# Eight adaLN modulation blocks: from TensorE in the attention to VectorE in the input projection

## The chip, the cores and the metric

The kernel runs on one core of one Trainium2 chip. The metric is the time of one execution on the device in microseconds (us). A trace is the record of one execution by the hardware profiler; its times are counted from its first instruction.

## The reference, cut to what matters

Two layers work on 256 latent tokens (and 256 context tokens that layer 0 alone reads), with 2048 features, in float32. Each sub-layer is modulated and gated by six vectors of 2048 that come from the conditioning vector `c`:

```
m_lat = split(silu(c) @ ada_w[i] + ada_b[i], 6)      # ada_w[i] is 2048 x 12288, 100.7 MB
hn    = modulate(rms_norm(h, norm1_g[i]), m_lat[0], m_lat[1])
h     = h + m_lat[2] * mixer_or_conv(hn)             # layer 0: attention + RWKV-7, layer 1: convolution
h     = h + m_lat[5] * mlp(modulate(rms_norm(h, norm2_g[i]), m_lat[3], m_lat[4]))
```

In layer 0 the mixer projects `hn` with one 2048 x 6560 matrix (`mix_in_w`), runs eight attention heads and sixteen RWKV heads on the result, and projects back with `mix_out_w`. The product `silu(c) @ ada_w` has one row. It is made here in blocks of 512 columns, 24 blocks per layer; a block is 2048 x 512 weights, 4.19 MB. Blocks 8 to 15 of layer 0 are `m_lat[2]` (the mixer's gate) and `m_lat[3]` (the second shift).

## The kernel before, in words

The kernel is one hand-ordered program: each engine (TensorE, VectorE, ScalarE, GpSimd, SyncE) has its own list of instructions in a fixed order, and semaphores tie the lists together. SyncE's list (`block.sync`) issues the weight loads, in order.

**The input projection.** `mix_in_w` is cut into 13 matrices of 512 columns, m0 to m12 (the last has 416), and each into four chunks c0 to c3 of 512 rows (1.05 MB). This text calls one chunk of one matrix a slot and writes (m, c). For each slot SyncE loads the chunk into `raw`, ScalarE rounds it (`split_hi`, line 410), VectorE makes the rest (`split_lo`, line 422), and TensorE multiplies (line 445, 48 matmuls to a slot). m0 and m1 need two of the four token groups (24 matmuls a slot). m6 and m7 need only the 256 latent tokens, and so do the last rows of m12. The hi and lo buffers hold one matrix: the rounding of chunk c of matrix m+1 waits until TensorE has finished slot (m, c). In the code's loops over m and c, VectorE therefore does the split of (m+1, c) in its own slot (m, c), beside TensorE's slot (m, c+1). After its four slots VectorE empties PSUM banks 2 and 3 of matrix m to `stage` (line 2700), and ScalarE banks 0 and 1 (line 2557). From m4 on ScalarE then issues the four stores of `stage`; two of them wait for VectorE's copies, and the next rounding stands behind them in ScalarE's list.

**Modulation blocks on VectorE.** Sixteen blocks (layer 0's 16 to 23, then layer 1's 0 to 7; `ADA_M`) are made beside the projection. A block is 16 pieces of 128 x 512. SyncE loads a piece (`load_piece`, line 739) into one of six buffers (`piece`: four in `gate`, two in `tmpa`), and a buffer is free when VectorE has used the piece before. VectorE multiplies it by one scalar per partition and adds it to an accumulator in `line` (`piece_step`, lines 749 and 752). `STEP_RATE[m]` says how many pieces VectorE does behind the split in each slot of matrix m. When a block's 16 pieces are done, TensorE sums the accumulator over the partitions (`sum_rows`, four matmuls at line 713) into a PSUM bank of the next matrix's half, and ScalarE copies the row and stores it to `mod_scratch` in DRAM (`keep_rows`, lines 767 and 718). `M_SUM` gives the slot before which TensorE does this: the first one after the slot that follows the block's last piece, at c1 or c2. TensorE waits there for the pieces (`macc_ok`), in order with its products.

Where VectorE also works on q and k: for m0 to m3 it normalises and turns the rows (`turn_sums`, `turn_rows`) in the first slots of the matrix behind.

**Attention.** Eight heads follow, one per pass n of a loop, pipelined across the engines (`attention`). In pass n TensorE makes the scores of head n (line 2876), transposes the maps of head n-1 (2888), multiplies them with the values (2901), and transposes k and q of head n+1 (2863, 2866). VectorE takes the maxima (2718), copies half of the transposed maps (2745), and makes the maps (2731, 2737), the queries (2712) and the outputs (2750, 2754). ScalarE does the exponentials (2583), the other half of the maps (2591), keys (2575), squares and a root (2597, 2605). Between these, TensorE makes one modulation block per pass (`weights`, line 382: 16 matmuls from `raw`, four per chunk): blocks 8 to 15 of layer 0. Chunks 0 and 1 stand ahead of the transposes of the maps, chunk 2 ahead of the values, chunk 3 behind the transposes of k and q. ScalarE copies the four partial rows of each and stores them (`act_ada`, lines 400 and 402). SyncE loads one 1.05 MB chunk at a time, when TensorE has used the one before (line 368).

`PARTED` names the two vectors whose sums lie in DRAM as four partial rows: their readers (`load_mod_rows`, `gate_part`, on GpSimd's queue) load or add four rows and not one.

Of the kernel before, what the change touches and what calls it, by code (L numbers as in the profile page):

```python
# [20 lines left out]
NB = 512  # L21
# [108 lines left out]
MIX_M = 13  # L130
ADA_A, ADA_T = 8, 1
ADA_M, M_BUF = 16, 6
ADA_L, L_BUF = 16, 3
Q_AT = ADA_A
Q_ALL = Q_AT + ADA_T * HEADS
SCAN = [[0, 1, 2, 3], [1, 0, 3, 2]]
# [99 lines left out]
def build_trunk(nc, a, out):  # L236
    with ExitStack() as top:
# [88 lines left out]
        mrow_zero = sem("mrow_zero")  # L326
        PARTED = [(0, 2), (0, 3)]
        late_in = [sem(f"late_in{b}") for b in range(L_BUF)]
# [26 lines left out]
        def weight_src(mat, col, n=NB, row=0):  # L355
            return mat[bass.ds(row, D), bass.ds(col, n)].rearrange("(k p) n -> p k n", p=P)
# [302 lines left out]
        def gate_part(pool, n, l, c, g):  # L659

            pool.wait_ge(gate_in, GATE_END[n - 1] + (g + 1) * 16)
            if n == 0:
                pool.wait_ge(ada_st, 16 * 4)
            pool.dma_start(gate[:, :], mod_d[l, g:g + 1, c * D:(c + 1) * D].to_broadcast([P, D]), accum_op=ALU.add).then_inc(gate_in, 16)
# [41 lines left out]
        def mix_ada(b):  # L706

            return (0, (16 + b) * NB) if b < 8 else (1, (b - 8) * NB)

# [9 lines left out]

        STEP_RATE = [3, 1, 7, 4, 4, 8, 3, 3, 7, 7, 7, 8, 8]  # L720
        M_STEPS = [0]
# [4 lines left out]
        for b in range(ADA_M):  # L726
            t = next(j for j in range(len(M_STEPS)) if M_STEPS[j] >= (b + 1) * KT) + 1
            while t % NCH not in (1, 2) or t in M_SUM:
                t += 1
            M_SUM[t] = b  # L730
# [24 lines left out]
        def sum_rows(pe, m, c, b):  # L755

            pe.wait_ge(macc_ok, (b + 1) * KT)
            if m >= 1:
                pe.wait_ge(mix_ev_a, evacuated(m - 1, c - 1))
            pe_partition_sums(pe, mix_bank(m + 1, c - 1), macc[b % 3]).then_inc(mrow_ps, 1)  # L760
# [171 lines left out]
        def rwkv_pool(pool, first):  # L932
# [29 lines left out]
            gate_bias(pool, 0, 2)  # L962
            for g in range(4):
                gate_part(pool, 0, 0, 2, g)
# [1012 lines left out]
        def sync_rest(sp):  # L1977
            src = lambda m: ("product", m - 1)
            for e in range(4):
                send(sp, weight_src(w["out"], e * NB), NB, src(M_OUT + e) if e else ("ada", Q_ALL - 1))  # L1980

# [19 lines left out]
        def pool_rest(pool):  # L2001
            stage_end(pool, 3)

            pool.wait_ge(ada_st, 16 * HEADS)
            pool.wait_ge(mrow_st, 16 * ADA_M)
# [418 lines left out]
        def _(sp):  # L2424
# [26 lines left out]

            sp.wait_ge(hi_done, 4 * MIX_M)
            sp.wait_ge(lo_done, 4 * MIX_M)
            with sp.Fori(0, HEADS) as i:
                q = i + Q_AT
                send_ada(sp, 0, i * NB + Q_AT * NB, ("ada", q - 1))

# [53 lines left out]
        def _(act):  # L2511
# [96 lines left out]
            def attention(first_rates, first_decays, first_exponentials):  # L2608

                keys(0)  # L2610
                for n in range(HEADS + 1):
# [18 lines left out]
                    if n == HEADS:  # L2630
                        first_exponentials()
                    if n < HEADS:
                        act_ada(act, 0, (n + Q_AT) * NB, n + Q_AT, 0, n * 16, 0)
                    if n == HEADS - 1:
# [160 lines left out]
        def _(pe):  # L2795
# [82 lines left out]

            def weights(i, c):

                pe_ada_chunk(pe, i + Q_AT, i + (Q_AT + MIX_M), c, 0, i + Q_AT)

            def maps_turned(i):
# [28 lines left out]
            def attention(first_rates, first_decays, first_norm):  # L2912

                turned(0)
                for n in range(HEADS + 1):
                    if n < HEADS:
                        scores(n)
                    if n >= 2:
                        outputs_turned(n - 2)
                    if n < HEADS:  # L2920
                        weights(n, 0)
                        weights(n, 1)
                    if n:
                        maps_turned(n - 1)
                    if n < HEADS:
                        weights(n, 2)
                    if n == HEADS:
# [3 lines left out]
                    if n + 1 < HEADS:  # L2931
                        turned(n + 1)
                    if n < HEADS:
                        weights(n, 3)
                    if n == HEADS - 1:
# [29 lines left out]
```

## Time and profile before

| | us |
|---|---|
| runs, median of 3 | 3243.42 |
| runs, lowest and highest | 3241.31, 3244.7 |
| span of the profiled execution | 3244.1 |

The profile gives the span as the profiled execution's own time. Busy shares of the span: TensorE 93%, its weight loads 77%, VectorE 68%, ScalarE 38%, GpSimd 7%.

| stretch of the trace, us | what runs | TensorE busy, us |
|---|---|---|
| 122 to 606 | input projection m0 to m12 | nearly all |
| 614 to 741 | attention, and the eight blocks | 95.80 |
| 745 to 1249 | RWKV heads | 441.28 |
| from about 1290 | output projection, MLP, convolution, MLP | nearly all |

How to read it: busy time counts compute instructions alone; in brackets, behind "<-", stands what ended the idle time ahead of an instruction. A share over the whole span mixes stages with different limits, so each stretch is read by itself.

### The profile page before, as it was taken

The numbers are of one execution on the slowest core, as the hardware profiler recorded it, in microseconds if no ns is written. First come the engines' busy times: TensorE is split into PE (matmuls) and PEld (weight loads), VectorE is DVE, ScalarE is ACT, GpSimd is POOL, SyncE is SP. The second block draws the span as 40 slices with busy tenths as digits, with TensorE's granted clock in tenths as the row PEclk, the third lists the DMA queues.
The fourth block names the chain that finished last, engine by engine and source line by source line (L and its number), as shares of the span: only waits on it lengthen the run. The fifth ranks groups of instructions, "written<-read, shape, count | busy, mean of one in ns | idle before, by whom it ended". The sixth has DMA issues, their size and how long they took to land.

```text
span 3244.1 us, 49985 instructions
## 1 busy us (share of the span) xinstructions
PE 3021.5 (93%) x20896; PEld 2496.8 (77%) x20896; DVE 2202.5 (68%) x2736; ACT 1244.9 (38%) x1430; POOL 217.1 (7%) x394
## 2 busy tenths in 40 slices
PE   5899999778889888999999999999889999999999
PEld 2588987536677766788888888799867888888887
DVE  3677766477887885577777878759974555555554
ACT  1322221174444443344443434343643343434342
POOL 1000000001000000012122121100000000000000
PEclk9799999899999998999999999999989999999999
DMA  9976887790000033668888888756205455555553
GB/s 326 352 273 238 317 289 246 271 368 24 12 14 13 22 67 106 208 230 285 279 295 281 293 292 277 260 166 184 92 23 181 159 194 186 191 185 192 194 182 130
DMA packets 306013, 640.59 MB, mean 197 GB/s; under 512 B 19035, under 2 KB 23937, under 8 KB 303585
## 3 DMA queue, kind: packets, MB, share of 16 engines
q1 hardware_dynamic: 269280, 529.94, 48.3%
q0 software_dynamic: 28384, 94.76, 9.0%
q10 hardware_dynamic: 8128, 12.72, 1.1%
q8 instruction: 166, 2.72, 0.3%
q14 instruction: 55, 0.45, 0.0%
HBM read 623.81 MB, written 13.40 MB: 196 GB/s over the span
## 4 chain that ended last, share of the span: by engine, by line
PE 83%; DVE 9%; DMA 4%; issue 2%; ACT 2%; ACTq 0%; SPq 0%; POOLq 0%; DVEq 0%
PE ps L445 46%; PE ps L463 15%; PE ps L465 7%; DMA raw<-in_ada_w_dram 3%; PE ps L2385 2%; PE ps L1662 2%; DVE rw_scl L1336 1%; DVE rw_mb L1353 1%; PE ps L382 1%; PE ps L1820 1%; PE ps L1772 1%; DVE rw_mt L1356 1%; DVE rw_scc L1339 1%; PE ps L1569 1%; DVE line L752 1%
## 5 line engine op out<-in xcount | busy, mean ns | idle before, releaser
L422 DVE TENSOR_TENSOR split_lo<-raw,split_hi 128x2048 fp32r<-128x2048 f32 (+1 forms) x372 | 849.7, 2285 | 496.7 <-ACT split_hi L410 488.8
L410 ACT ACTIVATE split_hi<-raw 128x2048 fp32r<-128x2048 f32 x368 | 702.1, 1911 | 1180.4 <-PE ps L445 840.3
L463 PE MATMUL ps<-xa,split_hi 128*128 128x512 f32 x2048 | 723.4, 398 | 6.4 <-ACT xa L617 6.4
L465 PE MATMUL ps<-xa,split_lo 128*128 128x256 f32 x2048 | 574.0, 280 | 0.0
L463 PEld LDWEIGHTS ps<-xa,split_hi 128*128 128x128 f32 x2048 | 384.6, 188 | 103.0 <-ACT xa L617 7.4
L445 PE MATMUL ps<-split_hi,hT_hi 128*128 128x512 f32 x1024 | 399.6, 390 | 0.0
L445 PE MATMUL ps<-split_hi,hT_lo 128*128 128x512 f32 x1024 | 398.5, 389 | 0.0
L445 PE MATMUL ps<-split_lo,hT_hi 128*128 128x512 f32 x1024 | 398.4, 389 | 0.0
L465 PEld LDWEIGHTS ps<-xa,split_lo 128*128 128x128 f32 x2048 | 386.5, 189 | 0.2
L445 PEld LDWEIGHTS ps<-split_hi,hT_hi 128*128 128x128 f32 x1024 | 192.2, 188 | 41.4 <-issue 1.8
L445 PEld LDWEIGHTS ps<-split_hi,hT_lo 128*128 128x128 f32 x1024 | 192.2, 188 | 40.2
L445 PEld LDWEIGHTS ps<-split_lo,hT_hi 128*128 128x128 f32 x1024 | 192.2, 188 | 39.4
L445 PE MATMUL ps<-xa,split_hi 128*128 128x256 f32 x1024 | 184.6, 283 | 2.8 <-ACT xa L617 2.8
L445 PE MATMUL ps<-split_hi,xa 128*128 128x512 f32 x512 | 162.8, 398 | 18.2 <-ACT xa L2110 11.7
L1950 DVE SCALAR_TENSOR_TENSOR line<-line,cvec 128x512 f32<-128x512 f32 x160 | 120.0, 750 | 71.4 <-DMA line<-in_ada_w_dram 65.9
L445 PEld LDWEIGHTS ps<-xa,split_hi 128*128 128x128 f32 x1024 | 159.7, 192 | 3.3 <-ACT xa L617 3.3
L445 PE MATMUL ps<-mx_hi,split_hi 128*128 128x512 f32 (+1 forms) x448 | 158.6, 354 | 0.0
L445 PE MATMUL ps<-mx_hi,split_lo 128*128 128x512 f32 (+1 forms) x448 | 157.4, 351 | 0.0
L445 PE MATMUL ps<-mx_lo,split_hi 128*128 128x512 f32 (+1 forms) x448 | 157.4, 351 | 0.0
L445 PE MATMUL ps<-xa,split_lo 128*128 128x256 f32 x512 | 144.9, 283 | 0.0
L382 PE MATMUL ps<-raw,s 128*32 128x512 f32 x512 | 85.9, 765 | 63.0 <-DMA raw<-in_ada_w_dram 58.0
L1662 PEld LDWEIGHTS ps<-rw_zz,rw_mt 64*64 64x64 f32 x3072 | 100.3, 138 | 56.5 <-DVE rw_mt L1356 53.4
(386 smaller groups left out, 4521.1 us busy)
## 6 DMA issues: line engine op xcount, KB each, us to landing
raw<-in_mlp_w_dram SPq DMA_DIRECT2D x256, 1024.0 KB, 5.4
raw<-in_ada_w_dram SPq DMA_DIRECT2D x64, 1024.0 KB, 9.6
raw<-in_mix_in_w_dram SPq DMA_DIRECT2D x48, 1024.0 KB, 5.7
raw<-in_conv_pw_w_dram SPq DMA_DIRECT2D x48, 1024.0 KB, 5.4
gate<-in_ada_w_dram SPq DMA_DIRECT2D x172, 256.0 KB, 5.0
line<-in_ada_w_dram POOLq DMA_DIRECT2D x171, 256.0 KB, 5.1
late<-in_ada_w_dram POOLq DMA_DIRECT2D x85, 256.0 KB, 5.0
tmpa<-in_ada_w_dram SPq DMA_DIRECT2D x84, 256.0 KB, 4.9
```

Source lines behind the costliest of these rows:

```text
L382: mm = pe.matmul(ps[32 * kk:32 * kk + 32, ADA_ACC[acc], :], s32[:, c * CHUNK + kk, :], raw[:, c, kk, :], start=(c == 0), stop=(c == NCH - 1))
L410: nc.scalar.activation(split_hi[:, c, :, 0:n], raw[:, c, :, 0:n], ACT.Copy).then_inc(hi_done, 1)
L422: nc.vector.tensor_tensor(split_lo[:, c, :, 0:n], raw[:, c, :, 0:n], split_hi[:, c, :, 0:n], ALU.subtract).then_inc(lo_done, 1)
L445: mm = pe.matmul(dst, l, r, start=(first and i == 0 and opens), stop=(last and i == 2), skip_group_check=True)
L463: pe.matmul(ps[:, base + j, :], split_hi[:, c, kk, j * P:(j + 1) * P], both, start=(k == 0), stop=False, skip_group_check=True)
L465: mm = pe.matmul(ps[:, base + j, 0:SEQ], split_lo[:, c, kk, j * P:(j + 1) * P], xa_hi[:, k, :], start=False, stop=(k == KT - 1), skip_grou ...
L752: nc.vector.scalar_tensor_tensor(out=acc, in0=piece[n % M_BUF], scalar=scale, in1=acc, op0=ALU.mult, op1=ALU.add).then_inc(macc_ok, 1)
L1336: ins = V.tensor_tensor(rw["scl"][:, c - 2, inst, :].rearrange("p (q t) -> p q t", q=4), ps[:, SCB[n], :].rearrange("p (q t) -> p q t", q= ...
L1339: ins = V.tensor_tensor(rw["scc"][:, c, inst, :].rearrange("p (q t) -> p q t", q=2), ps[:, SCB[n], 0:2 * P].rearrange("p (q t) -> p q t", ...
L1662: mm = pe.matmul(ps[own_half(e), ZB[b], j * HB:(j + 1) * HB], R["mt"][own_half(e), b, j, :], R["zz"][own_half(e), b, j, :], start=False, s ...
L1950: nc.vector.scalar_tensor_tensor(out=acc, in0=lpiece[n % L_BUF], scalar=scale, in1=acc, op0=ALU.mult, op1=ALU.add).then_inc(macc_ok, 1)
L2385: mm = pe.matmul(ps[:, j // 2, (j % 2) * SEQ:(j % 2 + 1) * SEQ], diag[:, t % DIAG_SLOTS, j, :], gpad[:, KT - PE_F + j, t:t + SEQ], start=( ...
```

## The change

- All 24 blocks (`ADA_M` from 16 to 24) are made on VectorE during the projection; layer 0's blocks 8 to 15 come last. The 32 loads of 1.05 MB on SyncE's list, the 128 matmuls and the eight copies and stores of ScalarE in the attention are gone; 128 piece loads of 0.26 MB, 128 VectorE steps, eight partition sums and eight row copies with stores come in the projection.
- `STEP_RATE` goes from [3, 1, 7, 4, 4, 8, 3, 3, 7, 7, 7, 8, 8] to [3, 2, 8, 7, 7, 9, 10, 10, 11, 11, 12, 12, 0] pieces a slot.
- TensorE's sums may stand ahead of c1, c2 or c3 (before: c1 or c2). Ahead of c3 they use bank lane 2, which VectorE empties.
- `PARTED` is empty: each vector is one row in DRAM, loaded or added once. The first weights of the output projection wait for the last split of the projection, not for the last modulation block.

By the two lists and the rule of `M_SUM`, the number of pieces per matrix and the sums come out so (worked out from the code):

| | m0 | m1 | m2 | m3 | m4 | m5 | m6 | m7 | m8 | m9 | m10 | m11 | m12 |
|---|---|---|---|---|---|---|---|---|---|---|---|---|---|
| pieces before | 12 | 4 | 28 | 16 | 16 | 32 | 12 | 12 | 28 | 28 | 28 | 32 | 8 |
| pieces after | 12 | 8 | 32 | 28 | 28 | 36 | 40 | 40 | 44 | 44 | 48 | 24 | 0 |
| sums after | 0 | 1 | 1 | 2 | 1 | 2 | 3 | 2 | 3 | 3 | 3 | 3 | 0 |

```diff
-ADA_A, ADA_T = 8, 1
-ADA_M, M_BUF = 16, 6
+ADA_A, ADA_T = 8, 0
+ADA_M, M_BUF = 24, 6
-Q_ALL = Q_AT + ADA_T * HEADS
+Q_ALL = Q_AT + ADA_T
-        PARTED = [(0, 2), (0, 3)]
+        PARTED = []
@@ gate_part
-                pool.wait_ge(ada_st, 16 * 4)
+                pool.wait_ge(mrow_st, 16 * ADA_M)
@@ mix_ada
-            return (0, (16 + b) * NB) if b < 8 else (1, (b - 8) * NB)
+            if b < 8:
+                return 0, (16 + b) * NB
+            return (1, (b - 8) * NB) if b < 16 else (0, (b - 8) * NB)
@@ the rates and the places of the sums
-        STEP_RATE = [3, 1, 7, 4, 4, 8, 3, 3, 7, 7, 7, 8, 8]
+        STEP_RATE = [3, 2, 8, 7, 7, 9, 10, 10, 11, 11, 12, 12, 0]
-            while t % NCH not in (1, 2) or t in M_SUM:
+            while t % NCH == 0 or t in M_SUM:
@@ sum_rows
-                pe.wait_ge(mix_ev_a, evacuated(m - 1, c - 1))
+                pe.wait_ge(mix_ev_a if c < 3 else mix_ev_d, evacuated(m - 1, c - 1))
@@ sync_rest, and the loads on SyncE's list
-                send(sp, weight_src(w["out"], e * NB), NB, src(M_OUT + e) if e else ("ada", Q_ALL - 1))
+                send(sp, weight_src(w["out"], e * NB), NB, src(M_OUT + e))
-            with sp.Fori(0, HEADS) as i:
-                q = i + Q_AT
-                send_ada(sp, 0, i * NB + Q_AT * NB, ("ada", q - 1))
@@ ScalarE's attention
-                    if n < HEADS:
-                        act_ada(act, 0, (n + Q_AT) * NB, n + Q_AT, 0, n * 16, 0)
@@ TensorE's attention
-                        weights(n, 0)
-                        weights(n, 1)
...
-                        weights(n, 2)
...
-                        weights(n, 3)
```

## Rows read from the trace of the kernel before

**Rows 1.** Busy time by stretch: us, busy by engine (instructions), granted clock, DMA share.
```profile
344.00:370.00 26.00, 26.00 (x219) 25.51 (x219) 18.93 (x21) 10.12 (x8) 0.00 (x0) 1.00 0.82 288
440.00:484.00 44.00, 44.00 (x207) 35.62 (x206) 29.72 (x35) 8.96 (x8) 0.00 (x0) 1.00 0.80 283
606.00:728.00 122.00, 87.53 (x566) 40.46 (x565) 76.09 (x201) 65.64 (x144) 5.90 (x9) 0.89 0.95 342
```

**Rows 2.** Waits from 120 to 607: us in total, times, longest.
```profile
ACT split_hi L410 <- PE ps L445: 256.0, 35, 10.7
DVE split_lo L422 <- ACT split_hi L410: 71.6, 29, 4.2
DVE line L752 <- DMA gate<-in_ada_w_dram: 14.5, 12, 1.7
```

**Rows 3.** Timeline of VectorE, slot (8, 0): start, duration, what, idle before.
```profile
404.99 2.29 DVE L422 TENSOR_TENSOR split_lo<-raw,split_hi 128x2048 fp32r<-128x2048 f32 x1 [3.55 <-ACT split_hi L410]
407.20 3.31 DVE L752 SCALAR_TENSOR_TENSOR line<-gate,s,line 128x512 f32<-128x512 f32 x4
410.62 1.61 DVE L752 SCALAR_TENSOR_TENSOR line<-tmpa,s,line 128x512 f32<-128x512 f32 x2
413.65 0.75 DVE L752 SCALAR_TENSOR_TENSOR line<-gate,s,line 128x512 f32<-128x512 f32 x1 [1.42 <-DMA gate<-in_ada_w_dram]
416.46 2.29 DVE L422 TENSOR_TENSOR split_lo<-raw,split_hi 128x2048 fp32r<-128x2048 f32 x1 [1.45 <-ACT split_hi L410]
```

**Rows 4.** Line 749 of VectorE, first piece of a block: ns min/median/max.
```profile
L749 DVE TENSOR_SCALAR line<-gate,s x11: 479/481/483, 138.8 to 574.8; 128x512 f32<-128x512 f32 x11
```

**Rows 5.** Line 739 of SyncE: piece loads, issue to landing.
```profile
DMA to landing us min/median/max: 2.7/4.9/11.8
```

**Rows 6.** Timeline of VectorE, turning the rows with and without position tables.
```profile
165.79 0.25 DVE L833 RECIPROCAL hbuf<-hbuf 128x16 f32<-128x16 f32 x1
...
171.20 2.28 DVE L422 TENSOR_TENSOR split_lo<-raw,split_hi 128x2048 fp32r<-128x2048 f32 x1
...
180.80 2.29 DVE L422 TENSOR_TENSOR split_lo<-raw,split_hi 128x2048 fp32r<-128x2048 f32 x1 [3.19 <-ACT split_hi L410]
...
285.65 0.24 DVE L833 RECIPROCAL hbuf<-hbuf 128x16 f32<-128x16 f32 x1
...
288.34 1.21 DVE L825 TENSOR_REDUCE hbuf<-hbuf 128x16 f32<-128x1024 f32 x1
```

**Rows 7.** Timeline of VectorE, three slots of m4: each split waits for TensorE's slot.
```profile
269.60 2.29 DVE L422 TENSOR_TENSOR split_lo<-raw,split_hi 128x2048 fp32r<-128x2048 f32 x1 [4.15 <-ACT split_hi L410]
...
280.48 2.29 DVE L422 TENSOR_TENSOR split_lo<-raw,split_hi 128x2048 fp32r<-128x2048 f32 x1 [4.23 <-ACT split_hi L410]
...
291.95 2.29 DVE L422 TENSOR_TENSOR split_lo<-raw,split_hi 128x2048 fp32r<-128x2048 f32 x1 [2.40 <-ACT split_hi L410]
```

**Rows 8.** Timeline of ScalarE, roundings released by TensorE at the ends of m6, m7, m11, m12.
```profile
368.56 1.92 ACT L410 ACTIVATE split_hi<-raw 128x2048 fp32r<-128x2048 f32 x1 [2.40 <-PE ps L445]
...
392.14 1.92 ACT L410 ACTIVATE split_hi<-raw 128x2048 fp32r<-128x2048 f32 x1 [3.54 <-PE ps L445]
...
571.35 1.60 ACT L410 ACTIVATE split_hi<-raw 128x1664 fp32r<-128x1664 f32 x1 [9.12 <-PE ps L445]
...
606.50 1.08 ACT L2557 ACTIVATE hbuf<-ps 128x512 f32<-128x512 f32 x2 [16.57 <-PE ps L445]
```

**Rows 9.** Timeline of VectorE, its copies of m5 and the split behind them.
```profile
357.99 1.28 DVE L2700 COPY hbuf<-ps 128x512 f32<-128x512 f32 x2
361.67 2.29 DVE L422 TENSOR_TENSOR split_lo<-raw,split_hi 128x2048 fp32r<-128x2048 f32 x1 [2.40 <-ACT split_hi L410]
```

**Rows 10.** Waits from 607 to 745, in the attention.
```profile
DVE at_pT L2745 <- PE ps L2888: 13.0, 2, 9.8
```

**Rows 11.** Timeline of TensorE in the attention, 660 to 712.
```profile
661.07 1.99 PE L2876 MATMUL ps<-at_kT,at_qT 64*128 64x512 f32 x8
...
669.36 2.02 PE L2901 MATMUL ps<-at_v,at_pT 128*128 128x128 f32 x16 [0.37 <-DVE at_pT L2745]
...
676.73 1.92 PE L382 MATMUL ps<-raw,s 128*32 128x512 f32 x16 [1.25 <-ACT line L400]
...
681.25 2.05 PE L2901 MATMUL ps<-at_v,at_pT 128*128 128x128 f32 x16 [0.57 <-ACT at_pT L2591]
...
703.24 3.46 PE L382 MATMUL ps<-raw,s 128*32 128x512 f32 x16 [3.74 <-ACT line L400]
```

More of the change, by code:

```diff
@@ L962, in rwkv_pool @@
             gate_bias(pool, 0, 2)
-            for g in range(4):
+            for g in range(parts_of(0, 2)):
                 gate_part(pool, 0, 0, 2, g)
@@ L2002, in pool_rest @@
             stage_end(pool, 3)
-            pool.wait_ge(ada_st, 16 * HEADS)
             pool.wait_ge(mrow_st, 16 * ADA_M)
@@ L2450, in _ @@
                 load_piece(sp, k)
-            sp.wait_ge(hi_done, 4 * MIX_M)
-            sp.wait_ge(lo_done, 4 * MIX_M)
-            with sp.Fori(0, HEADS) as i:
-                q = i + Q_AT
-                send_ada(sp, 0, i * NB + Q_AT * NB, ("ada", q - 1))
             sync_rest(sp)
@@ L2877, in scores @@
                               A["kT"][h * HD:(h + 1) * HD, :], start=True, stop=True).then_inc(at_sc, 1)
-            def weights(i, c):
-                pe_ada_chunk(pe, i + Q_AT, i + (Q_AT + MIX_M), c, 0, i + Q_AT)
             def maps_turned(i):
@@ L2919, in attention @@
                         outputs_turned(n - 2)
-                    if n < HEADS:
-                        weights(n, 0)
-                        weights(n, 1)
                     if n:
                         maps_turned(n - 1)
-                    if n < HEADS:
-                        weights(n, 2)
                     if n == HEADS:
@@ L2932, in attention @@
                         turned(n + 1)
-                    if n < HEADS:
-                        weights(n, 3)
                     if n == HEADS - 1:
```

## The prediction

> **What bounds the kernel now.** I read the busy time by stretch first, then the waits of the projection, then VectorE's timeline there, and last the attention. In the projection TensorE is busy in every microsecond of the two stretches shown, one with 256-token products and one with 512-token products, while VectorE works 18.93 of 26 us and 29.72 of 44 us [rows 1]. The waits say the same: ScalarE's roundings wait 256.0 us for TensorE, VectorE's splits 71.6 us for those roundings, and pieces wait 14.5 us for the larger group of their loads [rows 2]. So TensorE sets the pace and VectorE trails it with slack. In the attention no engine is full: TensorE 87.53 and VectorE 76.09 of 122 us, but DMA share is 0.95 [rows 1]. That share looks like the bound and mostly isn't: in the later passes VectorE goes straight from the maxima to its copy of the maps, and only two of those copies waited for TensorE, 13.0 us together [rows 10].
>
> The change therefore takes work from a stretch where most of it is hidden and gives it to VectorE where the slack is small. The question is whether VectorE still trails.
>
> **What a slot costs.** TensorE: 10.88 us for a full slot, 11.47 with a partition sum (280.48 - 269.60 and 291.95 - 280.48), so a sum is 0.59 us [rows 7]. A slot of m6 or m7 is (392.14 - 368.56)/4 = 5.9 us with the sum in it [rows 8].
> VectorE: a split moves on after 2.2 us (407.20 - 404.99), the pieces behind it after (410.62 - 407.20)/4 = 0.855 us each, of which 0.75 is the step and the rest its wait for the step before [rows 3]. The first of a block takes 0.48 and the same gap, 0.585 [rows 4]; so 16 pieces are 15 x 0.855 + 0.585 = 13.4 us, 0.84 each. With six buffers the seventh piece in a slot comes late: it waited 1.42 us here [rows 3], as a load lands 4.9 us after its issue at the median [rows 5] and six pieces last only 5.1 us. Pieces 8 to 12 ride on that wait, and the split refills the buffers. Over the kernel before, such waits were 14.5 us in 12 cases in the one group [rows 2], 1.2 each, while some slots had none. I take 1.0 us for each slot of seven or more pieces, with bounds 0 (the refills keep up, as in the slots with fewer pieces) and 2.0 (more traffic).
>
> So a full VectorE slot with 10, 11 or 12 pieces is 2.2 + 0.84 n + 1.0 = 11.6, 12.4 and 13.3 us. TensorE's is 10.9 to 11.5, and 5.9 in m6 and m7. VectorE no longer trails; it leads. Since nearly every sum from m6 on stands two slots behind its pieces, TensorE then waits at the sums (`macc_ok`), with all its products queued behind, and ScalarE and SyncE queue behind those.
>
> **The sum for the projection.** I follow VectorE from its first split of stage m2 to its last piece, in slot (11, 1), the release of the last sum.
> - 364 pieces (m2 to m10 340, m11 24) x 0.84 = 305.8.
> - Splits: 36 x 2.2 and 2 x 1.8 for the narrower last matrix = 82.8.
> - Copies of the banks at each matrix's end, 1.28 and less when packed [rows 9]: nine, 7 x 1.2 + 2 x 0.7 = 9.8.
> - Turning of q and k. With position tables 171.20 - 165.79 = 5.4, without 288.34 - 285.65 = 2.7, and a sum of squares 1.1 to 1.2 each [rows 6]. m2 has one of each (6.5), m3 and m4 have 2.7 + 5.4 + 2.3 = 10.4: 27.3. The lambda arithmetic in m8: 1.
> - Load waits: 38 slots x 1.0 = 38.
> - A new stall. ScalarE's next rounding stands behind stores that wait for VectorE's copies of the matrix. Once VectorE leads, each matrix change costs it the 2.40 us that one already cost when it was late [rows 9]. m5 to m11: 7 x 2.4 = 16.8. Its lower bound is 0 if the rounding could run ahead, but its place in ScalarE's list excludes that.
> Together 481.5 us.
>
> Where it starts: VectorE's first split of stage m2 stood at 180.80 [rows 6]. The change puts the first sum ahead of (1, 3), and its sixteenth piece in VectorE's slot (1, 1). That slot's one piece was over by 165.8 [rows 6]; with one more there and one in (1, 0) it ends at 167.5. Going back from 180.80 by the rounding and one slot, TensorE entered (2, 0) at 167.9 and (1, 3) at 162.5, so it will wait some 5.2 us and then sum for 0.6. Start: 180.8 + 5.9 = 186.7, and VectorE's end 668.2. Then come the sum 0.6, slot (11, 3) 10.9, and m12, which took 606.50 - 571.35 = 35.15 [rows 8] and loses its two sums, 34.0. TensorE ends the projection at 713.7 and not at 606.5: **+107 us**. (The eight added sums cost TensorE 4.7 us, hidden in its waits.)
>
> As a check by totals: 128 pieces more are 107 us. The idle that could take them is at most 71.6 + about 24 of load waits [rows 2], and most lies in m3, m4 or ahead of splits where the pieces are now denser anyway.
>
> **The attention.** What goes: TensorE's 128 matmuls, their loads, ScalarE's copies (0.6 us and 0.5 of issue each). What was on the path: of VectorE's 13.0 us of waits for the maps, 9.8 in pass 1, behind a late weight chunk, and 3.2 in pass 6, behind ScalarE's copy [rows 10]. In pass 1 the scores still have to end first, so 8.5 of the 9.8; in pass 6 ScalarE's exponentials are next, 2.4. Two passes had their values 0.6 to 0.8 late (one of them is the row at 681.25 [rows 11]), 1.4 together, and the ScalarE copy ahead of the RWKV rates, 1.2. Sum -13.5. All other passes are a chain of maxima, map copy, values, squares, root and outputs, that holds none of the removed work.
>
> What it gives back: TensorE had the removed matmuls between its own. In pass 3 scores start at 661.07 and values at 669.36 [rows 11]; between them only 3.6 us of work is left (scores 2.0, transposes 1.5), so 4.7 us idle. Ahead of the row at 703.24 TensorE was idle 3.74 us, and its 16 matmuls then took 3.46 us, where the same 16 at 676.73 took 1.92 [rows 11]: half speed, 1.2 and not 2.4 GHz. After such a gap come the values, 2.0 us on the chain. From 0 to 7 x 2.0 = 14 us is given back; by the one case seen most gaps would do it, by phase not all. I take 5.5. **Attention: -8 us**, bounds -13.5 and +1.
> The Trainium skill, "TensorE: Matmul & The Clock Gate", Part 1 (The HAM clock gate), says that the clock falls to half after an idle stretch and returns under load; its "HAM oscillation" part warns that a kernel can pay this every iteration. By that rule every pass would pay: attention about 0 and the total some 8 us higher. The row at 703.24 agrees with the fall; no row shows it pass after pass.
>
> The rest: single rows instead of four on GpSimd's queue, and the earlier load of `mix_out_w`, lie under the RWKV stage (504 us) at no cost; without that cover a few us.
>
> **Total.** Against the profiled span 3244.1: +107 - 8 = +99, 3343. The median of the runs is 0.7 us lower: 3243.4 + 99 = **3342 us**.
>
> **Rivals.**
> - A, VectorE leads but loads keep up (wait 0 per slot): 107 - 38 = +69, and the attention at its best, -13.5: 3299. For it: loads below seven pieces a slot never waited. Against: 1.42 us in the row shown.
> - B, DMA becomes the bound. A slot with 12 pieces moves 1.05 + 12 x 0.262 = 4.2 MB; at the 283 GB/s of 440 to 484 [rows 1] that is 14.8 us, 11 pieces 13.9 and 10 pieces 13.0, against 13.3, 12.4 and 11.6. Over 38 slots about 1.2 more: +45, 3387. For it: that stretch already had a share of 0.80. Against: the attention moved 342 GB/s [rows 1].
> - C, VectorE's idle takes the steps, and the attention's saving decides: faster, 3243 - 13.5 = 3230. It decides if VectorE's mean slot stays below TensorE's. Against: in m6 and m7 11.6 us stand against 5.9, and lateness can't be won back, since TensorE has no idle time.
> - D, the clock gate takes every pass (above): 3350, inside the forecast's range.
> - E, no gain and no loss: the steps fit and the saving is eaten. 3243.
>
> **Chances.** Forecast with D (3315 to 3365) 0.62; A 0.16; B 0.16; C 0.03; E 0.03. The range 3287 to 3392 holds A's and B's centres and leaves out their far halves, C and E. A measurement of this kernel tells 0.2% (6.5 us) from no change. Faster 0.03, same 0.03, slower 0.94.
>
> **What would show it.** The projection's end (ScalarE's L2557 of m12) near 714; waits of L713 for VectorE's L752 of 80 us or more in sum, largest in m6 and m7; L752 waiting for loads 30 to 45 us; VectorE's split behind each copy from m5 on idle some 2.4 us. The attention from its first transposes to the RWKV rates 8 us shorter, with values (L2901) that take 3 to 4 us in some passes. I am wrong if TensorE stays busy through m6 and m7, if L752's waits for loads are near zero or above 80, or if the attention shortens by 20 or more.

## The result, and the profile after

The kernel after takes 3374.6 us (median of 4 runs, 3369.0 to 3378.0) against 3244.1 for the kernel before beside it: a ratio of 1.040, interval 1.039 to 1.042. It is slower by 130 us; the forecast was 3342, in a range (3287 to 3392) that holds the measured time. The time lies above the band of 3315 to 3365 that the prediction gave to its own reading, and nearer to rival B's 3387 than to 3342; so the number by itself does not speak for the mechanism, and the trace and the runs below have to. Its profiled span is 3367.3 us, against 3244.1, a difference of 123; the steps below go by it.

The span falls into four stretches at instructions that both kernels have: ScalarE's last copy of m12, TensorE's first transposes of the attention, its transpose of the RWKV values, and the first product behind the RWKV stage.

| us | before | after | difference | forecast |
|---|---|---|---|---|
| projection, to m12's copy | 606.5 | 732.9 | +126.4 | +107 |
| from there to the attention | 7.6 | 8.2 | +0.6 | 0 |
| attention | 130.8 | 131.7 | +0.9 | -8 |
| RWKV stage | 527.8 | 523.3 | -4.5 | 0 |
| rest | 1971.4 | 1971.3 | -0.1 | 0 |

Busy time of the kernel after by stretch, first m6 and m7, then the attention, with the columns of [rows 1]:

```profile
393.00:495.00 102.00, 67.73 (x431) 60.63 (x430) 77.24 (x93) 18.31 (x19) 0.00 (x0) 0.81 0.87 302
741.00:873.00 132.00, 76.09 (x359) 56.51 (x360) 85.80 (x212) 69.19 (x155) 6.11 (x9) 0.72 0.18 61
```

Before, TensorE was busy in every microsecond of the projection's two stretches in [rows 1]. Now VectorE is the fuller engine in m6 and m7, and TensorE is idle for a third. The attention moves 61 GB/s where it moved 342, with a DMA share of 0.18 for 0.95, and is no shorter. Its granted clock is lower, 0.72 for 0.89. The one wait for a late weight chunk, in pass 1, did go (below); the six passes behind it, taken together, got no shorter without the transfers.

The waits of the projection after, the counterpart of [rows 2]:

```profile
ACT split_hi L410 <- PE ps L445: 291.1, 31, 20.9
ACT split_hi L410 <- DVE hbuf L2694: 106.9, 7, 21.4
PE ps L715 <- DVE line L754: 76.0, 15, 16.0
DVE split_lo L422 <- ACT split_hi L410: 46.3, 13, 11.5
DVE line L754 <- DMA gate<-in_ada_w_dram: 45.6, 36, 5.7
PE ps L445 <- ACT line L769: 19.1, 8, 2.4
ACT hbuf L2553 <- DMA qkv_scratch<-hbuf: 19.0, 2, 10.3
DVE line L754 <- DMA tmpa<-in_ada_w_dram: 13.5, 10, 2.8
```

The third row is TensorE at the sums (L715 is before's L713, L754 its L752): 1.6 us before, 76.0 now, 31.8 of it in m6 and m7. Pieces wait 59.1 us for loads (45.6 and 13.5). The second is ScalarE's rounding kept behind stores whose copies VectorE has not made. The sixth was not foreseen: a matrix's first product waits for ScalarE's copy of the summed row (L769), eight times 2.4 us.

VectorE's timeline, as in [rows 6], [rows 9] and the ends of [rows 8]: the first split of m2, the copies of m4 and the split behind them, the last pieces, and the split of (11, 3); then ScalarE's copy that ends the projection.

```profile
192.49 2.29 DVE L422 TENSOR_TENSOR split_lo<-raw,split_hi 128x2048 fp32r<-128x2048 f32 x1 [10.77 <-ACT split_hi L410]
...
340.43 1.28 DVE L2694 COPY hbuf<-ps 128x512 f32<-128x512 f32 x2
344.12 2.29 DVE L422 TENSOR_TENSOR split_lo<-raw,split_hi 128x2048 fp32r<-128x2048 f32 x1 [2.41 <-ACT split_hi L410]
...
683.94 1.61 DVE L754 SCALAR_TENSOR_TENSOR line<-tmpa,s,line 128x512 f32<-128x512 f32 x2
...
698.86 1.89 DVE L422 TENSOR_TENSOR split_lo<-raw,split_hi 128x1664 fp32r<-128x1664 f32 x1 [11.51 <-ACT split_hi L410]
```

```profile
732.89 1.08 ACT L2553 ACTIVATE hbuf<-ps 128x512 f32<-128x512 f32 x2 [32.20 <-PE ps L445]
```

TensorE's timeline: the first sum, in front of (1, 3); m12's first product; and in one pass of the attention, for [rows 11], the turning and the values:

```profile
166.53 0.65 PE L715 MATMUL ps<-line,ones_t 128*32 128x128 f32 x8 [5.83 <-DVE line L754]
...
699.24 0.47 PE L445 MATMUL ps<-mx_hi,split_hi 128*128 128x512 f32 x1 [2.11 <-ACT line L769]
...
770.82 0.71 PE L2878 MATMUL ps<-ident_t,at_p 128*128 128x128 f32 x5
777.00 3.40 PE L2891 MATMUL ps<-at_v,at_pT 128*128 128x128 f32 x16 [5.47 <-ACT at_pT L2587]
```

The values took 2.02 us at 669.36 before [rows 11]; here 3.40, behind 5.47 us of idle time in which they waited for ScalarE's copy of the turned maps.

One thing more stands in TensorE's rows around the first sum. Behind the 5.83 us of waiting its granted clock is lower:

```profile
166.50:170.00 3.50, 3.48 (x15) 2.51 (x16) 3.40 (x7) 0.00 (x0) 0.00 (x0) 0.50 1.05 386
167.90:178.85 10.95, 10.95 (x56) 8.80 (x55) 9.65 (x10) 2.52 (x2) 1.08 (x2) 1.00 0.86 305
```

The first row is after, the second is slot (2, 0) before. At 0.50, which is 1.2 GHz, the products of 512 columns follow each other every 0.43 us, at 1.00 every 0.23.

### The profile page after: what moved, and what is told of

The parts are those of the page before. It is cut to its first block, busy times and chain, and to the rows that moved or that the text cites. A ratio compares the mean times of both kernels' runs of the same rounds, so it can differ in the third digit from the quotient of the medians.

```text
span 3367.3 us, 49833 instructions
## 1 busy us (share of the span) xinstructions
PE 3027.6 (90%) x20704; PEld 2517.9 (75%) x20704; DVE 2294.4 (68%) x2864; ACT 1240.9 (37%) x1430; POOL 213.2 (6%) x388
## 3 DMA queue, kind: packets, MB, share of 16 engines
q1 hardware_dynamic: 270816, 529.94, 46.3%
## 4 chain that ended last, share of the span: by engine, by line
PE 65%; DVE 8%; issue 1%; ACT 1%; DVEq 0%; ACTq 0%
PE ps L445 32%; PE ps L463 14%; PE ps L465 7%; PE ps L2386 2%; PE ps L1664 2%; DVE rw_scl L1338 1%; DVE rw_mb L1355 1%; PE ps L1822 1%; PE ps L1774 1%; DVE rw_mt L1358 1%; DVE rw_scc L1341 1%; PE ps L1571 1%; PE ps L1590 1%; DVE tmpa L604 0%; PE ps L1787 0%
## 5 line engine op out<-in xcount | busy, mean ns | idle before, releaser
L754 DVE SCALAR_TENSOR_TENSOR line<-gate,s,line 128x512 f32<-128x512 f32 x240 | 180.2, 751 | 64.7 <-DMA gate<-in_ada_w_dram 45.6
L445 PE MATMUL ps<-split_hi,xa 128*128 128x512 f32 x512 | 162.9, 398 | 18.5 <-ACT xa L2111 11.7
L445 PE MATMUL ps<-mx_hi,split_hi 128*128 128x512 f32 (+1 forms) x448 | 166.8, 372 | 11.8 <-ACT line L769 11.8
```

The lines of the kernel that those rows point to most:

```text
L445: mm = pe.matmul(dst, l, r, start=(first and i == 0 and opens), stop=(last and i == 2), skip_group_check=True)
L754: nc.vector.scalar_tensor_tensor(out=acc, in0=piece[n % M_BUF], scalar=scale, in1=acc, op0=ALU.mult, op1=ALU.add).then_inc(macc_ok, 1)
```

## The experiments

Three questions: what makes up the projection's 126 us; why the attention gained nothing; and whether some part of the move is worth having. Times are medians; a difference from after is from 3374.6, and one from before goes by the ratio of the runs beside it.

### Projection: four single changes to the kernel after

**Loads once.** Only the first six pieces are ever loaded.

```diff
             if n >= M_BUF:
-                sp.wait_ge(macc_ok, n - M_BUF + 1)
+                return
```

> The kernel after, in which only the first six pieces of the modulation weights are loaded and VectorE reads those six buffers again and again (the blocks' values are not the reference's). Waits for loads are gone. If the working of the forecast is right, that they are worth their measured size and no more, the projection ends 38 to 59 us earlier than after's 732.9 and the kernel takes 3315 to 3337 us. If the transfers' slow share of the DMA engines set the whole loss, it falls to 3260 or below. If VectorE's work and the places of the sums set it and a wait merely shows where slack is, it changes by under 10 us.

Measured 3334.5 us, 40 less than after; the projection ends at 692.1, 40.8 earlier. No piece waits for a load any more, and this is what took the place of it:

```profile
DVE split_lo L422 <- ACT split_hi L410: 60.7, 19, 13.1
PE ps L715 <- DVE line L754: 47.0, 8, 14.7
PE ps L445 <- ACT line L769: 19.1, 8, 2.4
```

So 59.1 us of load waits were worth 41: the other 18 came back in part as splits that wait for roundings, 60.7 for 46.3. Rival B, that DMA sets the pace, would have had this kernel near the one before. It is 2.7% slower (ratio 1.027, 1.025 to 1.030) with 378 of 384 loads gone. Loads are 41 of the 126 us; for the rest VectorE's own work and what it is coupled to are left.

**Sums one chunk later.**

```diff
             t = next(j for j in range(len(M_STEPS)) if M_STEPS[j] >= (b + 1) * KT) + 1
+            t += 1
             while t % NCH == 0 or t in M_SUM:
```

> The kernel after with each block's partition sums one chunk later than now. If VectorE's throughput sets the stages, nothing changes but that the eight waits of a matrix's first group for the row copy (19.1 us in the trace of after) and the waits of sums for the last pieces go: -5 to -20 us against after. If the placement ahead of the fourth chunk is itself what stalls the projection, it gives back most of the loss: -60 us or more. If the move only puts the stall elsewhere: within 3 us.

Measured 3350.5 us, 24 less; the projection ends at 714.9, 18.0 earlier. VectorE's first split of m2 is at 182.8 for 192.5, of m11 at 655.7 for 661.7. So 9.7 us come at the start and 12.0 at the end, and the nine matrices between give 3.7 back. As I read it, VectorE is the bound between and a sum's place is nearly free there; at both ends TensorE is, and there a sum that comes before its last piece is done stops it. The waits for the row copy went from eight to five, 19.1 to 11.8 us.

**Stage stores on GpSimd.** They leave ScalarE's list, where its next rounding stood behind them.

```diff
-                for b, dst, r, t0 in mix_out(m) if m >= 4 else []:
-                    act.wait_ge(mix_ev_a if b < 2 else mix_ev_d, evacuated(m, b))
-                    act.dma_start(dst, stage[0:r, b, 0:TOK - t0]).then_inc(mix_st[b], 16)
...
+            for m in range(4, 10):
+                stage_stores(m)
```

> The kernel after with the stores of the projection's stages (m4 and later) issued by GpSimd instead of ScalarE, so that ScalarE's rounding of the next slot no longer stands behind a store that waits for VectorE's copy. Theory coupling: VectorE's splits behind the copies no longer wait 2.4 us in m5 to m11, and the wait of a first group for the row copy shrinks with it: -17 us, to -25 with the row copies. Theory throughput alone: VectorE waits for its piece loads in the same time instead, under -5 us.

Measured 3361.3 us, 13 less; the projection ends 11.4 earlier, and the gap in front of the attention is 3.2 longer. The split behind a copy starts at once:

```profile
588.24 1.28 DVE L2701 COPY hbuf<-ps 128x512 f32<-128x512 f32 x2
589.43 2.28 DVE L422 TENSOR_TENSOR split_lo<-raw,split_hi 128x2048 fp32r<-128x2048 f32 x1
```

The 2.4 us at each matrix end were the coupling, and worth less than the 17 us that they add up to. The row-copy wait did not shrink with it, as I had written: it stayed 19.1 us, eight times.

**Pieces dealt out otherwise.**

```diff
-        STEP_RATE = [3, 2, 8, 7, 7, 9, 10, 10, 11, 11, 12, 12, 0]
+        STEP_RATE = [3, 2, 8, 7, 7, 9, 3, 3, 12, 12, 12, 12, 14]
```

> The kernel after with the same number of pieces dealt out otherwise: 3 instead of 10 a slot in m6 and m7, where the mixed rows are turned, and 12 to 14 a slot in m8 to m12, so that m12, which took none, takes 56. Theory throughput: the pieces cost the same wherever VectorE is the bound, so only the 35 us of m12 in which VectorE had no pieces are gained: -15 to -30 us. Theory turning: a slot of m6 and m7 holds turns, splits and ten pieces at once and is dearer than their sum: -40 us or more. Rival: pieces at 12 a slot outrun the loads, and it is slower than after.

Measured 3344.3 us, 30 less; the projection ends 29.1 earlier. By VectorE's splits m6 and m7 together take 54.2 us for 100.8, which is 56 pieces fewer at 0.83; m8 to m10 take 178.6 for 167.0 and m11 and m12 80.6 for 71.2, so 21 of the 46.6 us come back. What stays is of the size of the 35 us of m12 that had no pieces, the upper end of the first theory. Turning, splits and pieces in one slot are no dearer than their sum.

**The three mends together**, with rates 3, 2, 8, 7, 7, 9, 6, 6, 11, 11, 11, 12, 12.

> The kernel after with all three mends together: each sum one chunk later, the stage stores on GpSimd, and pieces dealt out so that m12 has a share (3, 2, 8, 7, 7, 9, 6, 6, 11, 11, 11, 12, 12 a slot). Alone they took off 24, 13 and 30 us. If these are separate costs they add up: 3307 us. If they are faces of one shortage, VectorE's time, they overlap: the late sums gained in part at the end of the projection, where the new dealing gains too, and the sum of the three is 45 to 55: 3320 to 3330. In neither case is it faster than before.

Measured 3310.6 us, 64.0 less than after, where the three alone were 24.1 + 13.2 + 30.2 = 67.5. They add up, within what the dealing of the pieces leaves open (it is not the same here as in the single run), so the reading that they are faces of one shortage was wrong. What is left of VectorE's waits:

```profile
DVE line L755 <- DMA gate<-in_ada_w_dram: 43.3, 31, 4.2
DVE line L755 <- DMA tmpa<-in_ada_w_dram: 16.2, 12, 3.0
DVE split_lo L422 <- ACT split_hi L410: 3.0, 2, 2.7
```

VectorE waits for roundings 3.0 us in all, and the projection is still 65 us behind before's (671.9 for 606.5). What is left is the work of 128 more pieces and their 59.5 us of load waits; no run parts the two here. The kernel is 2.0% slower than before (ratio 1.020, 1.018 to 1.022).

### The attention by itself, and two cures

**The attention alone** is after's attention behind before's projection. In this kernel and the three behind it the eight blocks are made nowhere, so they time the attention and don't replace the kernel.

```diff
-ADA_M, M_BUF = 24, 6
+ADA_M, M_BUF = 16, 6
...
-            while t % NCH == 0 or t in M_SUM:
+            while t % NCH not in (1, 2) or t in M_SUM:
```

> The attention's part of the change by itself: the projection is as before (16 blocks on VectorE, the old rates and chunks), the attention is as after, and the eight blocks 8 to 15 of layer 0 are made nowhere (zeros stand in their place). If the attention's own cost is what the trace of after shows (131.7 us against 130.8 before, the gap in front of it +0.5, the rest of the kernel -4.6), this kernel takes 3241 us, 0.999 of before. If the attention of after is long only because the projection in front of it changed, it comes out at the forecast's 122.8 us and the kernel at 3231 us or less. In the first case the copies of the transposed maps by ScalarE come late in each pass, the values take 3.4 to 3.8 us, and the granted clock of the attention is near 0.72.

Measured 3243.9 us, ratio to before 0.9996 (0.9985 to 1.0008): all eight blocks out of the attention, and nothing gained. The cause lies in the attention.

**TensorE kept at work.**

```diff
                     if n:
                         maps_turned(n - 1)
+                    if 0 < n < HEADS:
+                        warm(0)
...
+            def warm(c):
+                pe.wait_ge(at_v_in, 16)
+                for kk in range(CHUNK):
+                    pe.matmul(ps[32 * kk:32 * kk + 32, 4, :], s32[:, c * CHUNK + kk, :], A["v"][:, c, 0:NB], start=True, stop=True)
```

> As attn_only (blocks 8 to 15 made nowhere), and in passes 1 to 7 TensorE does 16 matmuls of no use (the zero columns of s32 by the values at_v, into bank 4) where the blocks' matmuls stood, 12 ahead of the turning of the maps and 4 behind the values. Theory clock: the attention lost its gain because TensorE, with nothing to do between a pass's scores and its turning, goes at half clock through the turning and the values: with the work of no use the values take 2.0 us again instead of 3.5, seven passes save 1.5 each and the scores and turns some 0.3 each, about -12 us against attn_only (3229). Theory table: it is ScalarE's loading of the Exp table behind the maxima, and TensorE's clock hides nothing: the matmuls of no use change nothing or cost what they delay, 0 to +4 us against attn_only.

**The Exp table loaded early.**

```diff
+                    if 0 < n < HEADS - 1 and n != 5 or n == HEADS - 1:
+                        nc.scalar.activation(A["st"][0:1, 60:61], epsc[0:1, 0:1], ACT.Exp)
```

> As attn_only (blocks 8 to 15 made nowhere), and behind the root of each pass ScalarE does an Exp of one element that waits for nothing, so that the Exp table is loaded while VectorE still takes the maxima. Theory table: the exponentials of the next pass start 1.3 us earlier, of which the chain through the last sum and VectorE's scaling gives back some 0.7 us a pass in at most six passes: -4 to -8 us against attn_only. Theory clock alone: the exponentials start earlier but TensorE's half-clock matmuls still set the pass; under -1 us.

**Both.**

> attn_only (blocks 8 to 15 made nowhere) with both aids: TensorE's matmuls of no use in passes 1 to 7, and ScalarE's one-element Exp behind each root but pass 5's. The two runs with one aid each took 1.5 and 2.6 us less than attn_only, 4.6 less and 3.1 more in their profiled spans. If the half clock and the late table load each hide the other's cure, since the values wait for whichever of the two copies of the turned maps is later and TensorE's turning comes before both, the two together bring passes 2 to 4 back to before's 11.9 us and the attention to about 120: 3234 to 3236 us. If neither is what holds the passes, it stays at 3241 or above.

| us | median | ratio to before | attention | start to first values | first to seventh values |
|---|---|---|---|---|---|
| before | | | 130.8 | 31.4 | 75.7 |
| after | 3374.6 | 1.040 | 131.7 | 22.0 | 84.4 |
| attention alone | 3243.9 | 0.9996 | 128.2 | 22.4 | 83.0 |
| kept at work | 3242.4 | 0.9988 (0.9979 to 0.9998) | 123.6 | 23.5 | 78.1 |
| table early | 3241.3 | 0.9985 (0.9976 to 0.9994) | 132.5 | 22.5 | 83.0 |
| both | 3239.5 | 0.9981 (0.9972 to 0.9990) | 125.5 | 23.2 | 75.2 |

Pass 1 gives back what was forecast, 31.4 to 22.4 us. The six passes behind it lose 7.4 of that. With TensorE kept at work the values run in 2.0 us in four passes, and 4.9 of the 7.4 are back. The early table alone changes nothing there, on top of the other it takes 2.9 more, and the six passes stand at 75.2 us where before had 75.7. By these profiles, one of each kernel, both are causes, and the clock hides the table. The timed gains are small, -1.5, -2.6 and -4.4 us against the attention alone, and the intervals of the four ratios overlap: the times agree with this reading and don't show it by themselves.

The end of the attention, from the seventh values on, took 22.7 and 22.0 us without the early Exp and 26.9 and 27.2 with it, so the whole attention is longer with it in both pairs (132.5 for 128.2, 125.5 for 123.6). A part of this is in the edit. It puts an Exp behind the root of pass 7 too, where no exponential follows: ScalarE loads the Exp table and at once the next one, and the RWKV rates start 3.7 us behind the root's start instead of 2.4. In the kernel with both, TensorE then waits 1.97 us for them instead of 0.60, and the last values take 3.6 us for 1.95. How much of the 4 to 5 us this is, no run shows.

How the table comes late. ScalarE in a pass of the kernel after, and then of the kernel with the early Exp (L2632):

```profile
767.74 1.28 ACT L2601 ACT_TABLE_LOAD   x1
769.03 0.30 ACT L2601 ACTIVATE at_st<-at_st,epsc 128x2 f32<-128x2 f32 x1
773.05 1.28 ACT L2579 ACT_TABLE_LOAD   x1 [3.73 <-issue]
774.35 0.69 ACT L2579 ACTIVATE at_e<-ps,at_st 128x512 f32<-128x512 f32 x1
```

```profile
642.81 0.30 ACT L2604 ACTIVATE at_st<-at_st,epsc 128x2 f32<-128x2 f32 x1
643.13 1.28 ACT L2632 ACT_TABLE_LOAD   x1
644.42 0.20 ACT L2632 ACTIVATE at_st<-epsc 1x1 f32<-1x1 f32 x1
646.81 0.69 ACT L2582 ACTIVATE at_e<-ps,at_st 128x512 f32<-128x512 f32 x1 [2.19 <-DVE at_st L2720]
```

In after ScalarE is idle for 3.73 us in front of the load, which starts when VectorE has the first maximum scaled (L2715, over at 772.98): here the wait of the exponential stands in front of the load. In the second kernel a one-element Exp that waits for nothing takes the load with it, and the exponential starts 0.92 us behind the start of the first maximum (645.89) instead of 2.24. Before, ScalarE's copy and store of the block's row stood between root and exponential, and the load ran right behind them, ahead of the wait:

```profile
663.47 1.28 ACT L2583 ACT_TABLE_LOAD   x1 [0.60 <-ACT line L400]
665.95 0.69 ACT L2583 ACTIVATE at_e<-ps,at_st 128x512 f32<-128x512 f32 x1 [1.19 <-DVE at_st L2721]
```

So a load does not always stand behind the wait of its activation. It does in the passes with nothing between root and exponential, also in the kernels with one or two blocks moved; why, no run shows.

The Trainium skill, "ScalarE: Activation LUTs", What ACT_TABLE_LOAD costs, gives 1283 ns for a load and some 1380 ns of drain beside it. The load agrees, 1.28 us in every row; of a drain no row here shows anything: the exponential starts 1.30 us after the load does, and the load at 643.13 follows the root's end by 0.02 us.

### Is a part of the move worth it?

Three kernels keep most blocks in the attention. **Two moved**, those of passes 1 and 6:

```diff
+KEPT = [0, 2, 3, 4, 5, 7]
...
-        STEP_RATE = [3, 1, 7, 4, 4, 8, 3, 3, 7, 7, 7, 8, 8]
+        STEP_RATE = [3, 1, 7, 5, 5, 9, 3, 3, 8, 8, 9, 9, 9]
...
-            while t % NCH not in (1, 2) or t in M_SUM:
+            t += 1
+            while t % NCH == 0 or t in M_SUM:
```

> The kernel before with two of the eight blocks moved, those of passes 1 and 6, where VectorE's removed work was dearest; six stay in the attention. The 32 added pieces lie at rates up by one in m3, m4, m5 and m8 to m12; each sum stands one chunk later than the first allowed. If pieces cost in the projection what the forecast's working priced (0.84 us each where nothing hides them) the projection grows by 16 to 27 us less what m12 hides, and the attention gives 8.5 + 2.4 us back: 3250 to 3260. If the projection's idle shares in m8 to m12 take them as the sum placement allows, the projection grows by under 2 us and the kernel comes to 3233.

Measured 3245.1 us, ratio 0.9996 (0.9987 to 1.0005): neither of my two cases. The projection grew by 8.1 us, the attention shrank by 5.4. The values came 20.4 us after its start, but the passes from first to seventh values took 80.2 for 75.7. The values took 3.7 and 3.5 us in passes 2 and 3 and 3.78 in pass 6, and in both passes without a block ScalarE was idle in front of the table load, 3.79 and 4.25 us.

**One moved**, that of pass 1, with the sums where before's rule puts them; rates 3, 1, 7, 4, 4, 8, 3, 4, 8, 8, 8, 8, 8.

> The kernel before with one block moved, that of pass 1; seven stay in the attention; rates up by one in m7 to m11 less what that needs, sums in the second and third chunk as before. The first values came 31.4 us after the attention's start before and 20.4 in the kernel with two moved, while its later passes kept their time only where their own block stayed. So the attention should fall to 120 to 122 us, from 130.8. The projection is bound by TensorE and pays for one more partition sum (0.6) and, if a sum waits for its last piece, 2 us: 3234 to 3238. Rival: the wait for the first weights comes back behind block 0 as it did with block 1, or the clock falls in pass 1 for want of its block, and the gain is under 3 us.

Measured 3258.2 us, ratio 1.0041 (1.0028 to 1.0054): slower with sixteen pieces than with thirty-two. The waits of its projection say why:

```profile
PE ps L719 <- DVE line L758: 12.2, 5, 3.5
```

Its projection grew by 14.2 us. Five sums, one in each of m8 to m12, stood one slot behind their last piece at a rate of 8 a slot, and stopped TensorE there. In the kernel with two moved every sum has a second slot, and the same row reads 2.1 us, once.

**One moved, with room.** The same block; each sum at least two slots behind its last piece and never in the fourth chunk, which costs rates of 4 and 5 in m6 and m7; and in pass 1 the two cures.

```diff
-        STEP_RATE = [3, 1, 7, 4, 4, 8, 3, 3, 7, 7, 7, 8, 8]
+        STEP_RATE = [3, 1, 7, 4, 4, 8, 4, 5, 8, 8, 8, 8, 8]
...
+            t += 1
             while t % NCH not in (1, 2) or t in M_SUM:
```

> Again one block moved, that of pass 1, but every sum stands at least two chunks behind the slot of its last piece, and only in the second and third chunk; and in pass 1, which has no block, TensorE does 16 matmuls of no use and ScalarE a one-element Exp. One block moved without this cost 14.2 us of projection, 12.2 of them five waits of sums for their last pieces, and gave 4.2 back in the attention, with the values of passes 1 and 2 at half clock. If the places of the sums made that cost and not the sixteen pieces, the projection ends at 607 to 609, and with the clock kept the attention takes 120 to 124 us: 3234 to 3240, the first whole kernel under before. If sixteen more pieces are themselves too many for VectorE, the projection still ends at 613 or later and the kernel takes 3245 or more.

Measured 3235.1 us, ratio to before 0.9971 (0.9961 to 0.9981). Its sums wait 0.9 us:

```profile
PE ps L719 <- DVE line L759: 0.9, 1, 0.9
```

Its projection ends at 606.0, no later than before's 606.5 with sixteen pieces and a sum more; the values of pass 0 come 21.0 us after the attention's start, and the attention takes 125.7 us. The profiled run took 3241.0 us, so the stretches explain 4.8 of the 9.5 us only. By the runs it beats the kernel before by 0.3%, and the kernel after by 4%. It changed the sums' places, the rates and the two aids at once, so the gain is that of the whole; what the sums' places alone give, with nothing moved, was not run.

## Why the prediction was right

The mechanism was: VectorE leads, TensorE waits at the sums. That is what the trace shows. The size was 99 us for 130, above the band of its own reading, and there is luck in how near it is: some terms are off both ways. By its own steps:

- **The start**, +5.9 forecast, is +11.7 (192.5 for 180.8). The wait at the first sum was 5.83 us for 5.2. Behind it came a wait that I had not foreseen, (2, 0)'s first product for ScalarE's row copy, 2.43 us, and the lower clock behind each of the two waits: slot (1, 3) took 8.1 us for 5.4 and slot (2, 0) 12.8 for 10.9, 4.6 together. Against that TensorE had reached the sum 1.8 us earlier than the working took it, 160.7 for 162.5. Two steps failed: I costed the sum in the fourth chunk and not what the next matrix waits for when a sum stands last, and I asked for the clock in the attention and put it at nothing in the projection.
- **VectorE from there to its last piece**, 481.5 forecast, is 493.1 (192.49 to 683.94 + 1.6). Single stages lie within 3.8 of their sums: m3 46.6 for 47.9, m6 and m7 50.9 and 49.9 for 49.5 each, m10 56.4 for 56.7. The sum is so near because its terms miss both ways. Load waits read 59.3 us in this stretch for 38, the step that was most mis-sized; waits for roundings 20.9 for 16.8; and the work itself, with its small gaps, 412.9 for 426.7. By experiment the loads are worth 41, near my value as a price, and the stalls at the matrix ends, 2.1 to 2.6 in every row, 11.4 or 13 of the 16.8 put in.
- **The tail**: from the last sum to m12, 13.6 us for 11.5; the difference is again the wait for the row copy, 2.11. m12 took 33.7 for 34.0.
- **The attention**, -8 forecast, is +0.9. Here the forecast failed in size and in cause. Pass 1's 8.5 came, as 9.0 to 9.5. Pass 6's 2.4 did not: passes 6 and 7 take 15.0 and 15.1 us for 15.4 and 12.4 before. The half clock was put at 5.5 us by one case; with TensorE kept at work 4.9 came back in the profile, so that term was about right. With all values at full clock it could have been more: three of the seven stayed slow in that kernel. The missing term is the table load: I removed ScalarE's copy and store from its list and asked only what they cost, and not what they had been standing in front of.
- **The rest**, 0, is -4.6, nearly all in the RWKV stage. The attention-alone kernel has -1.4 there and the early-table one -3.8. No run was made for its cause.

Of the signs that I named, the sum of TensorE's waits (76.0 us for 80 or more) and the load waits (59.1 for 30 to 45) missed, the first narrowly and the second by a third; the 2.4 us behind the copies are there.

Of the rivals, A and B go by the loads-once kernel: loads do not keep up, and they are not the bound, though B's number was the nearest. C asked for TensorE to stay busy in m6 and m7, and it was idle for a third; E asked for no change. D was right about the attention's time and about one of its two causes, and too small for the whole.

The Trainium skill, "TensorE: Matmul & The Clock Gate", HAM oscillation, says that a loop whose busy bursts are parted by waits can pay the cold clock in every turn. The trace agrees with it here: in each of the first seven passes of after the values take 3.4 to 3.8 us, behind 2.1 to 6.3 us of idle time. I gave the rule as rival D, inside the forecast's own chance; for the attention's time it was nearer than my sum.

## What to carry to other kernels

Before a background job moves to an engine that trails the bound by a third, add up the whole slot there and not the engine's mean share: VectorE was busy for 68 to 73% of the stretches and became the bound with ten pieces a slot. Give a consumer that sits in the critical engine's list a full slot of slack behind its producer: with that and pieces dealt out to fit, one moved block went from 14 us of loss in the projection to none. Keep it out of the last place before a hand-over, where it cost 2.4 us each time. And when work leaves an engine's list, look at what stood behind it, a table load that ran ahead, a clock that it kept up, and not only at what it cost.

## What the hardware showed that was not expected

- A table load can come behind the wait of its activation: ScalarE idle for 3.73 us, then 1.28 us of load, then the exponential. With a copy and a store in front of it, the load ran ahead of the wait. An activation of one element without a wait (0.20 us) brings the load forward.
- Two hidden costs in one chain, by one profile of each kernel: curing the table alone moved the six passes by 0.0 us, curing the clock alone by 4.9, both by 7.8.
- A wait at one sum costs more than the wait: behind 5.83 us without work TensorE ran at a granted clock of 0.50, and that and the next wait cost it 4.6 us in two slots.
- TensorE's matmuls of no use, 112 in seven passes, cost 1.1 us ahead of the first values and bring the granted clock of the attention from 0.71 to 0.86.
- DMA share says little of a bound: 0.95 at 342 GB/s in the attention before, 0.18 at 61 GB/s after, at nearly the same length; only pass 1 had gained from the transfers' end.
